# A hybrid attention block on one core: scaling over 128 partitions in eight groups, four score banks and two for maxima, scores four steps ahead

## The reference

```python
h = _rms_norm(x, norm_g) * (1.0 + scale) + shift
qa, ka, va, fa, za, qb, kb, vb, zb, ga, gb = split(h @ w_in)
log_f = log_sigmoid(fa + b_forget)                    # per head and token
# branch A: 8 heads x 64, causal; F = cumsum(log_f)
logits = q @ k.T * 64 ** -0.5 + F[t] - F[s]
ya = (softmax(causal(logits)) @ va * silu(za)) @ w_o_fox
# branch B: 8 query heads, 2 key heads, a window of 128 in chunks of 64, ALiBi, sinks
yb = (softmax([logits_b, sink])[:-1] @ vb * silu(zb)) @ w_o_swa
x = x + gate * ((sigmoid(ga) * ya + sigmoid(gb) * yb) @ w_out)
```

## Time and profile before

| | us |
|---|---|
| median of 3 runs | 2205.91 |
| lowest and highest of them | 2197.71, 2218.35 |
| the profiled execution | 2219.62 |
| its span, first to last instruction | 2217.90 |
| in it: before the first gather of attend | 1147 |
| attend's 382 steps | 1147 to 1818.8 |
| from there to the first load of merge | 1818.8 to 1832.6 |

### The profile page before, as it was taken

One profiled execution on the slowest core, in us unless ns is written; L12 is line 12 of the kernel. 1 busy time (PEld: TensorE's weight loads), 2 busy tenths in 40 slices (PEclk: granted clock), 3 DMA queues, 4 the chain that ended last, 5 costly groups with the idle time before them and its releaser, 6 DMA issues. The chain is left out here.

```text
span 2217.9 us, 28286 instructions
## 1 busy us (share of the span) xinstructions
PE 2037.9 (92%) x9722; PEld 1615.4 (73%) x9722; DVE 980.5 (44%) x1915; ACT 755.8 (34%) x1439; POOL 568.6 (26%) x534
## 2 busy tenths in 40 slices
PE   7489999999999999999869989989989977998998
PEld 2367878788788788888746666666666747998887
DVE  1945555652221400000054556577566645564332
ACT  1622222220121412212137666667666662101100
POOL 0610000000000000000017556566576562120000
PEclk9589999999999999999959889899998988999999
DMA  6233343444321212211172643534534315232222
GB/s 228 95 98 105 104 123 94 135 141 105 119 86 47 64 68 85 85 47 66 57 159 63 140 104 75 130 89 105 127 92 107 83 28 191 85 124 95 95 99 81
DMA packets 230057, 222.98 MB, mean 101 GB/s; under 512 B 53618, under 2 KB 187634, under 8 KB 227380
## 3 DMA queue, kind: packets, MB, share of 16 engines
q1 hardware_dynamic: 218180, 181.74, 29.5%
q0 software_dynamic: 11648, 39.85, 5.7%
q10 hardware_dynamic: 128, 0.13, 0.0%
HBM read 149.58 MB, written 72.09 MB: 100 GB/s over the span
## 5 line engine op out<-in xcount | busy, mean ns | idle before, releaser
L1017 POOL TENSOR_TENSOR Pl<-PT,Ph 128x512 fp32r<-128x512 f32 (+2 forms) x382 | 431.5, 1146 | 278.7 <-ACT Ph L1152 261.4
L454 PE MATMUL pj<-hTh,Wh 128*128 128x512 f32 x768 | 299.5, 390 | 0.6 <-DVE Wl L646 0.2
L455 PE MATMUL pj<-hTl,Wh 128*128 128x512 f32 x768 | 298.8, 389 | 0.0
L456 PE MATMUL pj<-hTh,Wl 128*128 128x512 f32 x768 | 298.8, 389 | 0.0
L454 PE MATMUL pj<-Wh,hTh 128*128 128x512 f32 (+1 forms) x640 | 246.3, 385 | 23.7 <-DVE Wl L646 23.6
L365 POOL DMA_DIRECT2D wraw<-in_w_in x84 | 45.1, 537 | 857.1 <-DVE Wl L646 851.2
L1145 ACT ACTIVATE PT<-sc 128x512 f32<-128x512 f32 (+2 forms) x382 | 199.0, 521 | 162.8 <-PE sc L1073 60.3
L455 PE MATMUL pj<-Wl,hTh 128*128 128x512 f32 (+1 forms) x640 | 240.2, 375 | 0.0
L456 PE MATMUL pj<-Wh,hTl 128*128 128x512 f32 (+1 forms) x640 | 240.1, 375 | 0.0
L1233 DVE TENSOR_REDUCE part_max<-mx 128x1 f32<-128x512 f32 (+3 forms) x288 | 169.0, 598 | 115.1 <-PE mx L1042 114.3
L1152 ACT ACTIVATE Ph<-PT 128x512 fp32r<-128x512 f32 (+2 forms) x382 | 214.3, 561 | 12.1
(11 more groups left out here) (214 smaller groups left out, 3647.7 us busy)
## 6 DMA issues: line engine op xcount, KB each, us to landing
qk_scratch<-qThl SPq DMA_DIRECT2D x96, 256.0 KB, 2.8
wraw<-in_w_in POOLq DMA_DIRECT2D x88, 256.0 KB, 3.9
g_scratch<-st SPq DMA_DIRECT2D x64, 256.0 KB, 2.4
gt<-g_scratch SPq DMA_DIRECT2D x16, 1024.0 KB, 7.8
xin<-in_x POOLq DMA_DIRECT2D x16, 512.0 KB, 4.7
wada<-in_w_ada SPq DMA_DIRECT2D x8, 1024.0 KB, 7.7
z_scratch<-st SPq DMA_DIRECT2D x32, 256.0 KB, 2.4
Qb<-qk_scratch SPq DMA_DIRECT2D x32, 256.0 KB
```

Of the source, the lines that this page charges most:

```text
L454: nc.tensor.matmul(out, a_hi, b_hi, start=first, stop=False)
L455: nc.tensor.matmul(out, a_hi, b_lo, start=False, stop=False)
L456: return nc.tensor.matmul(out, a_lo, b_hi, start=False, stop=last)
L1017: pool.tensor_tensor(Pl[n % NPH][0:rows, 0:w], PT[n % NP][0:rows, 0:w], Ph[n % NPH][0:rows, 0:w].bitcast(F32), ALU.subtract).then_inc(low_ ...
```

## The change

- NSC 4, NMX 2, NP 5, NPH 5, AHEAD 4. The due steps of the loads of keys and queries move one step ahead with AHEAD.
- The stationary operand that yields the results' second half and the sums has 65 columns (OUT) in place of 128; V, VA, VB and pick shrink with it, and so do the memsets.
- Blocks are grouped by where their results lie in yT: `place` gives a group k (of 8) and a place m (of 4). A group holds the f blocks of two heads at the same two quarters j and the s blocks of one head, 8 blocks. The heads of a pair lie in the two halves of the partitions, so that `scale` handles two f blocks or two s blocks in one product of 128 x 512: 4 products a group, three steps apart from 13 steps after the turn. The turns are at step 18 of heads 1, 3, 5 and 7 and at step 4 of heads 2, 4 and 6, and after the last step; the first products are due at step 31 and at step 17 of these heads.
- The scratch tensors take the new order; an s block's sums are stored in four pieces.

```diff
@@ -782,9 +782,10 @@
-    NSC, NMX, NP, NPH = 3, 3, 3, 4
+    NSC, NMX, NP, NPH = 4, 2, 5, 5
+    VW, OUT = 2 * HD + 4, HD + 1
...
-    AHEAD = 3
+    AHEAD = 4
@@ -822,37 +823,35 @@
-    batches, e0 = [], 0
-    for size in [8] * 7 + [6, 2]:
-        batches.append((e0, size))
-        e0 += size
+    place = lambda kind, i: (i // 8 * 2 + i % JB // 2, i % JB % 2) if kind == "f" else (i // 4, 2 + i // 2 % 2)
+    members = [[e for e, b in enumerate(blocks) if place(*b)[0] == k] for k in range(8)]
...
-    for e, size in batches:
-        turns.append(max(last[blocks[e + size - 1]] + 5, free))
-        free = turns[-1] + 13 + size
+    for units in members:
+        turns.append(max(last[blocks[units[-1]]] + 5, free))
+        free = turns[-1] + 24
...
-    scale_at = when(((k, e), n + 13 + m) for k, n in enumerate(turns) for m, e in enumerate(range(batches[k][0], sum(batches[k]))))
-    TAIL = 22
+    scale_at = when(((k, m), n + 13 + 3 * m) for k, n in enumerate(turns) for m in range(4))
+    TAIL = 28
...
-        V = sb("V", [P, TT, 3 * HD], F32R)
+        V = sb("V", [P, TT, VW], F32R)
...
-        pick, rs = sb("pick", [HD + 4, P], F32R)[:], sb("rs", [P, 32])
+        pick, rs = sb("pick", [HD + 4, OUT], F32R)[:], sb("rs", [P, 32])
...
-        VA = [sb(f"VA{k}", [P, KV_H, 3 * HD], F32R) for k in range(2)]
-        VB = [sb(f"VB{k}", [HD, KV_H, 3 * HD], F32R) for k in range(2)]
+        VA = [sb(f"VA{k}", [P, KV_H, VW], F32R) for k in range(2)]
+        VB = [sb(f"VB{k}", [HD, KV_H, VW], F32R) for k in range(2)]
@@ -975,23 +974,19 @@
-                    e0, size = batches[k]
-                    for e in range(sum(batches[k]) - min(size, NZ), sum(batches[k])):
+                    for e in members[k][-NZ:]:
...
-                        sp.wait_ge(scaled, e0)
-                    sp.dma_start(rs[0:16 * size, :], dram["sums"][e0:e0 + size].rearrange("e (a n) -> (e a) n", n=32)).then_inc(r_in, 16)
+                        sp.wait_ge(scaled, 4 * k)
+                    sp.dma_start(rs[:], dram["sums"][k].rearrange("m s (a n) -> (m s a) n", n=32)).then_inc(r_in, 16)
...
-                    e0, size = batches[k]
...
-                        rows = dram["inv"][e0:e0 + size].rearrange("(i k) n -> k i n", k=2)[half]
-                        sp.dma_start(R[half * HD:(half + 1) * HD, 0:size // 2, :],
-                                     rows.unsqueeze(0).to_broadcast([HD, size // 2, QW])).then_inc(r_in, 16)
+                        sp.dma_start(R[half * HD:(half + 1) * HD, :, :],
+                                     dram["inv"][k, :, half].unsqueeze(0).to_broadcast([HD, 4, QW])).then_inc(r_in, 16)
...
-                    e0, size = batches[k]
...
-                    sp.dma_start(dram["inv"][e0:e0 + size].rearrange("e (a n) -> (e a) n", n=32), rs[0:16 * size, :]).then_inc(inv_out, 16)
+                    sp.dma_start(dram["inv"][k].rearrange("m s (a n) -> (m s a) n", n=32), rs[:]).then_inc(inv_out, 16)
@@ -1003,10 +998,10 @@
-            pool.memset(V[:, :, P:3 * HD].bitcast(F32), 1.0).then_inc(ready, 1)
+            pool.memset(V[:, :, P:P + 1].bitcast(F32), 1.0).then_inc(ready, 1)
...
-                pool.memset(VA[k][:, :, P:3 * HD].bitcast(F32), 1.0).then_inc(ready, 1)
-                pool.memset(VB[k][:, :, P:3 * HD].bitcast(F32), 1.0).then_inc(ready, 1)
+                pool.memset(VA[k][:, :, P:P + 1].bitcast(F32), 1.0).then_inc(ready, 1)
+                pool.memset(VB[k][:, :, P:P + 1].bitcast(F32), 1.0).then_inc(ready, 1)
@@ -1108,12 +1103,12 @@
-                        nc.tensor.matmul(part(slice(0, P)), pick, QBa[t % 2][0:HD + 4, g * GH:(g + 1) * GH, :], start=True, stop=False)
+                        nc.tensor.matmul(part(slice(0, OUT)), pick, QBa[t % 2][0:HD + 4, g * GH:(g + 1) * GH, :], start=True, stop=False)
...
-                nc.tensor.matmul(part(slice(0, P)), values[:, HD:3 * HD], high, start=opening and kind == "f", stop=False)
+                nc.tensor.matmul(part(slice(0, OUT)), values[:, HD:HD + OUT], high, start=opening and kind == "f", stop=False)
...
-                nc.tensor.matmul(part(slice(0, P)), values[:, HD:3 * HD], low, start=False, stop=closing).then_inc(pv_done, 1)
+                nc.tensor.matmul(part(slice(0, OUT)), values[:, HD:HD + OUT], low, start=False, stop=closing).then_inc(pv_done, 1)
@@ -1165,7 +1160,13 @@
-                act.dma_start(dram["sums"][e:e + 1], sums[e % NZ]).then_inc(sum_out[e % NZ], 16)
+                kind, i = blocks[e]
+                k, m = place(kind, i)
+                if kind == "f":
+                    act.dma_start(dram["sums"][k, m, i // JB % 2:i // JB % 2 + 1], sums[e % NZ]).then_inc(sum_out[e % NZ], 16)
+                else:
+                    act.dma_start(dram["sums"][k, m, :, i % 2 * 2 * P:(i % 2 + 1) * 2 * P].rearrange("s (a n) -> a s n", n=P),
+                                  sums[e % NZ].rearrange("o (a s n) -> o a s n", s=2, n=P)).then_inc(sum_out[e % NZ], 16)
@@ -1207,8 +1208,8 @@
-                st.settle(nc.vector.memset(pick[HD:HD + 4, HD:P].bitcast(F32), 1.0))
-                nc.vector.memset(pick[HD:HD + 2, HD:P].bitcast(F32), 0.0).then_inc(ready, 1)
+                st.settle(nc.vector.memset(pick[HD:HD + 4, HD:OUT].bitcast(F32), 1.0))
+                nc.vector.memset(pick[HD:HD + 2, HD:OUT].bitcast(F32), 0.0).then_inc(ready, 1)
@@ -1273,17 +1274,19 @@
-                rows = 16 * batches[k][1]
...
-                nc.vector.reciprocal(rs[0:rows, :], rs[0:rows, :]).then_inc(inverted, 1)
-
-            def scale(k, e):
-                half, m = e % 2, (e - batches[k][0]) // 2
+                nc.vector.reciprocal(rs[:], rs[:]).then_inc(inverted, 1)
+
+            def scale(k, m):
...
-                dve.wait_ge(y_done, e + 1)
-                for out, r in zip(out_of(e), parts_of(e, R[half * HD:(half + 1) * HD, m, :])):
-                    last_op = nc.vector.tensor_tensor(out, out, r, ALU.mult)
-                last_op.then_inc(scaled, 1)
+                dve.wait_ge(y_done, members[k][-1] + 1)
+                if m < 2:
+                    j = k % 2 * 2 + m
+                    y, r = yT[:, k // 2, j * QW:(j + 1) * QW], R[:, m, :]
+                else:
+                    t = 2 * k + m - 2
+                    y, r = yT[:, 4:8, t * P:(t + 1) * P], R[:, m, :].rearrange("p (a n) -> p a n", n=P)
+                nc.vector.tensor_tensor(y, y, r, ALU.mult).then_inc(scaled, 1)
@@ -1294,8 +1297,8 @@
-                for k, e in scale_at(n):
-                    scale(k, e)
+                for k, m in scale_at(n):
+                    scale(k, m)
@@ -1562,8 +1565,8 @@
-        "sums": scratch("sums", [FOX_H * 8, COLS]),
-        "inv": scratch("inv", [FOX_H * 8, COLS]),
+        "sums": scratch("sums", [FOX_H, 4, 2, COLS]),
+        "inv": scratch("inv", [FOX_H, 4, 2, COLS]),
...

```

## The result

The changed kernel takes 2181.85 us, the median of four runs (2170.57 to 2184.46), against 2204.43 us (four runs) before: a ratio of 0.9872, 95% interval 0.9833 to 0.9912, so 1.3% less. On a second chip it came to 0.9849 (0.98 to 0.9899). The forecast was 2191 us, and the time lies in its range. The profiled execution took 2184.46 us with a span of 2182.7, which is 35.2 us under that of before. It was forecast 15.3 under, so some terms of the sum were wrong, and the question is which. By the medians the kernel gained 22.6 us: the profiled execution of before stood 15.2 us above its median, that of the changed kernel 2.6.

A forecast was written before the change was run, and what follows sets the result against it. Bound in attend: PE, held up by DVE's twelve back-to-back scale products, with the clock falling behind. Terms: -36.6 + 14.6 + 12.8 + 3.4 - 8 - 3.7 + 2.2 = -15.3 us, from 2205.9 to 2191 us; range 2157 to 2224.

The forecast's parts named there:

- The old scaling goes: Attend, heads 1 to 7: dropping the batches of twelve DVE scale products saves 36.6 us (bounds -30 to -37).
- The new scaling comes: Attend: 32 products of 128 x 512 cost 14.6 us, 11.4 of it in heads 1, 3 and 5 (bounds 3 to 25).
- Two banks for maxima: Attend, mainly j = 1 and j = 3: PE's third maxima item waits for DVE's read, +12.8 us (bounds 5 to 20).
- Four steps ahead: Attend: one more step of lead into j = 2, at most 1.3 us a head, -8 us in all (bounds -12 to 0).
- 65 columns: Attend: shorter weight loads for gathers behind a 128-column product such as the mask, -3.7 us (bounds -7 to 0).
- The clock: Attend: bank waits add one half-clock spell of 6.7 us, worth +3.4 us (bounds -10 to +30).
- rival B: Two banks for maxima bring two more half-clock spells in each of seven heads: 2235 us, slower; chance 0.12.
- The end: After attend's last step: no products before the sums' load, a longer load of R, four products: +2.2 us (bounds -1 to +6).
- SP's order: Heads' starts: keys and queries issued one step earlier, before rows of maxima also needed earlier: 0 us (bounds -3 to +10).
- rival C: Heads' starts: the row of maxima is needed 1.3 us earlier but comes no earlier, spells lengthen: 2215 us; chance 0.13.
- Rival A: Attend: DVE has room in j = 3 and the new waits are mostly hidden: 2168 us; chance 0.27.
- signs named ahead: Attend: no 1.75 us first-gather waits; some 10 us maxima-bank waits; steps 16 to 45 47 to 49 us even heads, 50 to 53 odd.

The follow-up runs named there:

- before_keys: The kernel before with only the load of a head's keys due 14 steps later: 2190.81 us, ratio 0.9911.
- scaling_keys: The kernel before with the new scaling and the load of keys due later; 128 columns and old banks stay: 2146.84 us, ratio 0.9711.
- best_keys: The kernel before with new scaling, 65 columns and the load of keys due later; old banks, places and lead of three: 2139.39 us, ratio 0.9662.
- best_thin: best_keys with each scaling product cut to one column, so almost all scaling is left out: 2130.92 us, ratio 0.964.
- after_nmx3: The changed kernel with three score banks, three banks for maxima and a lead of three; five places stay: 2174.29 us, ratio 0.983.
- after_nmx2_ahead3: The changed kernel with scores three steps ahead; four score banks, two for maxima and five places stay: 2184.37 us, ratio 0.9877.
- keys_later: The changed kernel with the load of a head's keys due 14 steps later: 2154.57 us, ratio 0.9738.
- after_again: The changed kernel run once more on a second chip, no edit: 2177.49 us, ratio 0.9849.
- scaling_cols: The changed kernel with the old banks, places and lead of three, so only scaling and 65 columns are new: 2171.92 us, ratio 0.9804.
- after: The changed kernel itself, against the kernel before: 2181.85 us, ratio 0.9872.
- rings_cols: The kernel before with 65 columns and the new banks, places and lead of four, but the old scaling: 2232.17 us, ratio 1.0082.

## Why the prediction was right, and where it was not

**What bounds the kernel** was read rightly. Twelve products in a row on DVE made the first gather of j = 3 wait and the clock fall behind it. With the scaling changed and nothing else (`scaling_alone`), steps 16 to 45 of heads 1 to 6 fell from 315.9 to 286.7 us and those of head 7 by 2.3.

**The old scaling goes, -36.6.** Right in size, and the clock is a large part of it. `before_keys` and `scaling_keys` differ by 4.8 or 4.9 us in heads 1 and 2, and 0.1 to 1.0 of new cost must be added: 5 to 6 us, where 5.6 were taken. The other differences are 6.1 us in heads 3 and 5, and 12.9 in heads 4 and 6. There the old wait of 1.76 us had the clock down not for 6.7 but for some 27 us, which ate 17 of the 39 us that the first 16 steps of heads 1 to 6 had gained from the later keys; see the last section.

**The new scaling comes, +14.6.** This step failed. The 11.4 us for heads 1, 3 and 5 are 0.1 to 0.2 us a head. Steps 30 to 45 of head 3, in `best_keys` and then in `best_thin`:

```profile
1412.57:1440.57 28.00, 25.38 (x123) 17.48 (x122) 18.85 (x52) 19.30 (x38) 19.02 (x17) 1.00 0.31 73
```
```profile
1406.78:1434.64 27.86, 25.40 (x123) 17.47 (x122) 16.93 (x53) 19.33 (x38) 18.57 (x17) 1.00 0.29 70
```

I had each product hold the maxima up by as much as 1.7 us. The timelines of DVE and POOL in the changed kernel, head 3, show them in DVE's gaps instead. They take 0.67 to 0.69 us where they start while POOL is idle, and 1.09 us where POOL is in the middle of a product with 0.54 us to go:

```profile
1441.17 0.67 DVE L1289 TENSOR_TENSOR yT<-yT,R 128x512 f32<-128x512 f32 x1
...
1446.42 1.09 DVE L1289 TENSOR_TENSOR yT<-yT,R 128x512 f32<-128x512 f32 x1
...
1452.45 0.68 DVE L1289 TENSOR_TENSOR yT<-yT,R 128x512 f32<-128x512 f32 x1
...
1458.83 0.69 DVE L1289 TENSOR_TENSOR yT<-yT,R 128x512 f32<-128x512 f32 x1
```
```profile
1445.67 1.29 POOL L1012 TENSOR_TENSOR Pl<-PT,Ph 128x512 fp32r<-128x512 f32 x1 [1.01 <-ACT Ph L1147]
```

The Trainium skill (SBUF — State Buffer, "SBUF: two separate sides") says that DVE, with two inputs in SBUF, and GpSimd hold a shared pair of ports in turn, each for a whole instruction. The trace agrees: the second product starts at 1446.42, POOL's ends at 1446.96, and the product is longer by 0.4 us, about that overlap.

The wait for R taken at 0.9 us is not there. The 0.8 us for a group in j = 2 was about right: steps 16 to 27 of head 4 take 17.3 us in `best_keys` against 16.3 in `best_thin`. The group in head 7 was taken at 0.8 us too and costs nothing (20.2 us for its steps 30 to 45 in both). DVE has nothing else to wait for in j = 2, so it takes the four products back to back there, three steps apart in the plan or not:

```profile
1324.03 4.68 DVE L1289 TENSOR_TENSOR yT<-yT,R 128x512 f32<-128x512 f32 x4
```

That is 1.17 us each on average: the first two take 0.69 us, the last two 1.77 and 1.78, since they start with 1.2 us of a POOL product to go. In both places a product that starts in the middle of one of POOL's ends 0.55 us after POOL's does.

**Two banks for maxima, +12.8.** Right for attend. From `after_nmx3` to `after_nmx2_ahead3`, heads 1, 3, 5 and heads 2, 4, 6 lose 1.9 and 1.4 us from step 6 on (measured in heads 5 and 6), head 0 loses 0.8 (to step 45) and head 7 0.3: 11.0 us, where 10.8 were laid out by hand. Heads 5 and 6, whose steps from 6 on no spell of half clock reaches in either run, stand for the others. One wait was missing in that layout: among a head's first four steps PE waits 1.0 us for a transposing's bank, so that they last 6.7 us in `keys_later` and 5.6 in `best_keys`. In the changed kernel it is hidden, since PE has waited for rows of QBa right before. With quiet starts it adds 1.1 us in each of seven heads.

**Four steps ahead, -8.** Right: 3 x 0.2 + 3 x 1.5 + 3.0 = 8.1 us from `after_nmx2_ahead3` to `after_again`. Heads 5 and 6 stand for the others here too. It is not spread as I had it, though: head 7 has the most. That the five places do nothing fits `after_nmx3`, whose steps 16 to 45 equal those of `scaling_cols` within 0.2 us.

**65 columns, -3.7.** Mis-sized, and past its bound of -7: it is 8.6 us. I counted only gathers behind a mask product. Those are there: starts 0.28 us apart in `scaling_keys`, then 0.23 in `best_keys`.

```profile
1450.17 0.27 PE L1070 MATMUL sc<-identr,maskr 128*128 128x128 f32 x1
1450.28 0.44 PE L1108 MATMUL ot<-Ph,V 128*128 128x512 f32 x1
1450.56 0.40 PE L1109 MATMUL ot<-Ph,V 128*64 128x512 f32 x1
```
```profile
1379.40 0.22 PE L1070 MATMUL sc<-identr,maskr 128*128 128x128 f32 x1
1379.46 0.39 PE L1108 MATMUL ot<-Ph,V 128*65 128x512 f32 x1
1379.69 0.39 PE L1109 MATMUL ot<-Ph,V 128*64 128x512 f32 x1
```

The same 0.05 us is saved at 62 products of 256 columns whose successor starts 0.17 instead of 0.22 us later, and where a gather ends on a narrow product and another follows.

**The clock, +3.4, and rival B.** In the changed kernel itself one spell of 3.4 us was new (head 0, whose clock is 0.96 above), worth 1.7 us. The mechanism behind the +3.4 did not bring it: it stands behind no wait for a bank but behind head 0's wait for `collect`, which the lead of four makes longer (2.2 us in `after` and `after_again`, 1.5 without a spell in `after_nmx2_ahead3` and `best_keys`; `keys_later` has 2.2 without one, so the wait alone is not the whole cause).

```profile
1176.57 0.41 PE L1108 MATMUL ot<-Ph,V 128*65 128x512 f32 x1 [2.22 <-DVE yT L1273]
```

With quiet starts the rival's mechanism shows in part. `best_keys`, with three banks, holds the full clock from 1151 us to the end of attend:

```profile
1151.00:1734.00 583.00, 548.01 (x2622) 362.73 (x2621) 317.60 (x786) 440.19 (x876) 414.17 (x378) 1.00 0.44 107
```

`keys_later` has four spells, 24 us together, worth about 12 of the 17.6 us. Two (6.8 us each) stand right behind a wait of 1.0 us for a bank. The other two (6.8 and 3.4 us) stand behind one of 1.4 and 1.0 us for rows in block j = 2, which is no matter of banks: with the lead of four PE takes these rows 2.0 us after their issue, where `best_keys` leaves them 2.9 to 5.0. One of each, first the timeline rows of PE, then the stretches:

```profile
1334.11 0.77 PE L1078 MATMUL sc<-QBa,KBa 66*128 66x512 f32 x1 [1.38 <-DMA QBa<-shift_b]
...
1455.67 0.50 PE L1037 MATMUL mx<-Ka,Qa 66*128 66x512 f32 x1 [1.04 <-DVE shift_rows L1228]
```
```profile
1456.30:1463.10 6.80, 6.80 (x22) 4.79 (x20) 3.08 (x8) 4.27 (x7) 4.47 (x4) 0.51 0.90 190
...
1333.50:1340.30 6.80, 6.19 (x18) 4.21 (x19) 0.00 (x0) 2.44 (x5) 3.99 (x5) 0.51 0.23 61
```

The rule cited in the prediction (the Trainium skill, TensorE: Matmul & The Clock Gate, "A second HAM failure mode: psum-queue depth-cycling") fits two of these four spells; `rings_cols` is another case, with one long idle stretch (5.7 to 6.2 us) in each of heads 2 to 6. It did not decide the change, whose gain of 1.3% stands. That the bank waits cause the two spells is inferred from their place: no run takes these waits away and keeps the lead and the places. Each of heads 1 to 7 has such a wait of 1.0 to 1.1 us at its start, and behind five of the seven no spell came.

**The end, +2.2** measured 2.5. **SP's order, 0**: the waits for QBa's rows grew from 11.8 to 17.9 us, at the heads' starts from 1.3 to 1.7 us each to 2.3 to 3.0, which is the step that rival C named. Yet the first 16 steps of heads 1 to 7 summed to about 217 us both before and after: the spells at heads' starts were 65 us before and 55 in this execution, and 24 in `after_again`, whose waits are as long. So rival C's waits came and its price did not, in part by chance, and the place that it named was worth as much as the whole change.

**The sum.** With the measured terms, scaling -31.5, banks and lead 11.0 - 8.1 = +2.9, columns -8.6, end +2.5, it is -34.7. The forecast had -22.0, +4.8 and +3.4 for the clock, -3.7 and +2.2. The profiled executions differ by 35.2, of which 5.2 the other way are outside attend and its end (4.2 before it, 1.0 in merge and output), so some 6 us are left that no term names. Two executions of the changed kernel differ by twice that in attend alone (627.8 us above, 615.6 in `after_again`), by the spells at the heads' starts. So the time came within 9 us of the forecast partly by luck: the sum was 20 us off in the profiled executions and 7 by the medians, with its two mis-sized terms (scaling, columns) both too cautious, and the range of 67 us held that. Rival A was right on its first reason (DVE has room in j = 3) and wrong on its second (the banks' waits are not hidden); the time came between it and the forecast. Of the signs named ahead, the waits of PE (7 us) and PEld (14 us) before L1037, for which some 10 were named, the missing 1.75 us waits of heads 1 to 6, the loads of 0.14 us and the even heads at 47 to 49 us came true. The 50 to 53 us for heads 1, 3 and 5 did not.

## What to carry to other kernels

Before pricing a burst of work that is moved into gaps, lay it into the engine's own timeline: four products of mostly 0.7 to 1.1 us with 5 to 6 us between their starts cost 0.1 to 0.2 us, twelve in a row cost a stall and the clock. A large prefetch that is due many steps later should not be issued just ahead of a small transfer that PE waits for: moving 1.5 MB by 13 steps was worth 1.4% here, as much as the whole change. A bank taken from one ring for another must be paid for by what the other ring gains. Here it never was: banks, places and lead together cost 0.7 to 0.8% with a prompt reader and 1.5% with a slow one.

## What the runs showed of the hardware

A wait of one length was followed by very different spells. In `before_keys`, head 4, the gather waits 1.76 us for `collect` and a transposing 1.21 us after it; in the earlier trace rows nearly the same pair cost 6.7 us at half clock, here 27 us, although PE had no other wait of more than 0.2 us in it. A timeline row of PE, then the stretch:

```profile
1507.73 0.79 PE L1113 MATMUL ot<-Ph,V 128*128 128x512 f32 x1 [1.76 <-DVE yT L1272]
...
1511.02 0.37 PE L1029 MATMUL mx<-ident,nmax 128*4 128x128 f32 x1 [1.21 <-DVE nmax L1242]
```
```profile
1506.00:1534.00 28.00, 25.06 (x60) 16.93 (x60) 11.63 (x35) 11.61 (x21) 10.80 (x9) 0.52 0.06 20
```

The other heads of the same execution make it no clearer. Head 6 is as head 4. Head 1 has waits of 1.79 and 1.21 us and then 6.8 us at half clock, heads 2, 3 and 5 have 1.77 and 1.9 to 2.0 and also 6.8, and head 7 has one wait of 2.2 us and no spell: the length of the waits alone does not set that of the spell. Why it lasted so long stays open. It is part of why the later keys gave the kernel before only 0.9%, and 1.4% once the scaling was changed (0.985 to 0.9711, and 0.9804 to 0.9662). Apart the new scaling gave 1.5% and the later keys 0.9%, together 2.9%. Both act through the clock, and the spells that one leaves eat into the gain of the other.
